# Step sizes and forget gates as fp32 products on four places of 32 columns, and the scan's heads later and further apart

## The reference, cut to what matters

```python
def mamba2_mixer(x, ln_g, in_w, conv_w, conv_b, dt_bias, a_log, d_skip, norm_g, out_w):
    zxbcdt = rms_norm(x, ln_g) @ in_w            # 1024 -> 5152 columns, the last 32 are dt
    z = zxbcdt[..., :D_INNER]
    xbc = zxbcdt[..., D_INNER:D_INNER + SSM_CONV_DIM]
    dt = zxbcdt[..., D_INNER + SSM_CONV_DIM:]
    xbc = jax.nn.silu(causal_dwconv(xbc, conv_w, conv_b))
    ...
    dt = jax.nn.softplus(dt + dt_bias)
    a = dt * (-jnp.exp(a_log))
    y = ssd_chunked(xs32 * dt[..., None], a, bm, cm)     # 32 heads in 4 groups, chunks of 128
    y = (y + xs32 * d_skip[:, None]).reshape(b, s, D_INNER) * jax.nn.silu(z)
    y = rms_norm(y, norm_g)                              # per group
    return y @ out_w

def fox_branch(q, k, v, f_logit, f_bias):
    log_f = jax.nn.log_sigmoid(f_logit + f_bias)         # 8 heads
    c = jnp.cumsum(log_f, axis=1)
    ...
        logits = q @ k * scale + c_q - c_k               # causal softmax, then @ v
```

## Time and profile before

| what | us |
|---|---|
| median of 3 timed runs (2403.49 to 2405.24) | 2404.54 |
| the profiled execution | 2402.46 |
| its span | 2400.7 |
| TensorE busy (99%) | 2376.7 |
| VectorE busy (58%) | 1403.3 |
| ScalarE busy (44%) | 1052.5 |
| GpSimd busy (15%) | 370.8 |

### The profile page before, as it was taken

How to read it: one execution, slowest core, us unless ns; L and a number is a source line. 1 busy time by engine, 2 the same in 40 slices (tenths; PEclk the granted TensorE clock), 3 DMA queues, 4 the chain that set the end, 5 groups by cost and what they waited for, 6 DMA issues and landing times.

```text
span 2400.7 us, 29668 instructions
## 1 busy us (share of the span) xinstructions
PE 2376.7 (99%) x11556; PEld 1930.8 (80%) x11556; DVE 1403.3 (58%) x2203; ACT 1052.5 (44%) x1803; POOL 370.8 (15%) x297
## 2 busy tenths in 40 slices
PE   8999999999999999999999999999999999999999
PEld 6777888888888877788888877787788877888887
DVE  6778776763665678766456557534555445443343
ACT  6654564442444677644234334324443334322223
POOL 0352252210111000121012100001211001110011
PEclk9999999999999999999999999999999999999999
DMA  4632223223223221232332332231243322223222
GB/s 164 110 92 79 81 74 101 88 86 109 96 82 127 72 71 54 75 102 94 98 102 87 99 131 72 78 102 61 68 132 128 114 97 88 88 95 99 105 78 90
DMA packets 74844, 226.19 MB, mean 94 GB/s; under 512 B 8144, under 2 KB 12368, under 8 KB 74576
## 3 DMA queue, kind: packets, MB, share of 16 engines
q1 hardware_dynamic: 70272, 215.90, 27.5%
q10 hardware_dynamic: 4432, 8.39, 2.0%
HBM read 215.87 MB, written 8.39 MB: 93 GB/s over the span
## 4 chain that ended last, share of the span: by engine, by line
PE 62%; DVE 1%; issue 0%; ACT 0%; POOLq 0%; POOL 0%; DVEq 0%
PE bank L1189 60%; PE bank L1193 1%; DVE t L2073 0%; ACT t L1595 0%; DVE t L2070 0%; DVE t L2081 0%; DVE t L2077 0%; ACT t L1598 0%; DVE t L2563 0%; POOLq L2862 0%; POOL t L2641 0%; DVEq L2862 0%; DVE t L2409 0%; DVE t L2078 0%; DVE t L2569 0%
## 5 line engine op out<-in xcount | busy, mean ns | idle before, releaser
L1189 PE MATMUL bank<-t 128*128 128x512 f32 (+4 forms) x11130 | 2352.3, 377 | 16.7 <-DVE t L2073 7.8
L1189 PEld LDWEIGHTS bank<-t 128*128 128x128 f32 (+2 forms) x11130 | 1888.0, 185 | 450.2 <-issue 80.0
L1595 ACT ACTIVATE t<-t 128x1024 fp32r<-128x1024 f32 (+6 forms) x634 | 539.3, 861 | 645.4 <-PE bank L1189 276.1
L2070 DVE TENSOR_TENSOR t<-t 128x1024 fp32r<-128x1024 f32 (+6 forms) x686 | 624.1, 920 | 260.6 <-ACT t L1595 254.5
L2641 POOL TENSOR_TENSOR t<-t 128x512 f32<-128x512 f32 (+4 forms) x217 | 329.0, 1523 | 1543.9 <-ACT t L1598 558.7
L1598 ACT ACTIVATE t<-t 128x512 f32<-128x512 f32 (+6 forms) x610 | 367.4, 616 | 450.3 <-DVE t L2070 301.2
L2070 DVE TENSOR_TENSOR t<-bank,t 128x512 f32<-128x512 f32 (+4 forms) x412 | 276.0, 674 | 451.9 <-PE bank L1189 441.5
L2073 DVE SCALAR_TENSOR_TENSOR t<-t 128x512 f32<-128x512 f32 (+4 forms) x493 | 364.0, 748 | 103.4 <-ACT t L1598 63.8
L1595 ACT ACTIVATE t<-bank 128x512 f32<-128x512 f32 (+4 forms) x151 | 72.2, 498 | 167.0 <-PE bank L1193 145.2
L2644 POOL TENSOR_SCALAR t<-t 128x128 f32<-128x128 f32 (+3 forms) x64 | 41.1, 649 | 476.8 <-ACT t L1595 246.1
L2073 DVE SCALAR_TENSOR_TENSOR t<-bank,t 128x512 f32<-128x512 f32 x56 | 38.5, 687 | 67.3 <-PE bank L1189 67.3
(11 more groups left out here) (30 smaller groups left out, 52.9 us busy)
## 6 DMA issues: line engine op xcount, KB each, us to landing
t<-in_w SPq DMA_DIRECT2D x304, 512.0 KB, 3.3
t<-in_w SPq DMA_DIRECT2D x48, 384.0 KB, 3.0
t<-in_w SPq DMA_DIRECT2D x56, 320.0 KB, 2.9
t<-in_w SPq DMA_DIRECT2D x28, 256.0 KB, 2.7
tab<-t ACTq DMA_DIRECT2D x1, 2560.0 KB
t<-in_x SPq DMA_DIRECT2D x8, 256.0 KB, 5.3
t<-tab SPq DMA_DIRECT2D x8, 256.0 KB, 3.9
spill<-t ACTq DMA_DIRECT2D x1, 2048.0 KB, 8.7
```

The lines of the kernel that those rows point to most:

```text
L1189: return eng.matmul(out, lhs, rhs, start=start, stop=stop, skip_group_check=loose)
L1595: return eng.activation(out, in_, ACT.Copy, scale=scale)
L2070: return eng.tensor_tensor(out, a, b, o)
```

## The change

The two narrow products get a form of their own, `thin`: one unit of 32 columns in one tick. Its weights are multiplied by the norm's gain in one VectorE step (in `cut`), without a split; the moving operand is the unsplit activation. The eight blocks go as plain fp32 products to four places of 32 columns, each place summing two blocks. The four partial sums lie on 128 partitions; VectorE scales them all, and the four transposes of `d1` and `f1` become products with four stacked identities in `l4`, which sum the places and turn the result at once. For the forget gates 32 columns are loaded and 8 used. `dt` moves from ahead of `in(0, 2)` to ahead of `in(0, 5)`, `fg` from the front of the mix stage to behind `sq 3`.

The first pair of group 0 may start 14 ticks after `stb` instead of 10, and pairs are 4 ticks apart instead of 3. Silu is whole on ScalarE for all `in` tiles of groups 0 to 2, 18 instead of 9; the table with Silu and Tanh is loaded at `in(2, 0)`, the one with Exp and Tanh at the first pair of groups 0 and 2.

```diff
@@ Plan
+    def thin(self, key, name, c0, src, nk, norm):
+
+        g = Group(key, False, src, 0, [], nk, 0, 32, S, norm=norm)
+        b = self.main_bank()
...
+        u = self.unit(name, 0, nk, c0, 32)
+        self.thin_units[u] = key[0]
+        g.units.append((u, 0, nk))
+        self.put(Piece(g, 0, 0, nk, True))
...
-                self.once("pair", (g, p), lambda g=g, p=p: self.past("stb", g, 10)
-                          and (p == 0 or self.past("pair", (g, p - 1), 3)),
+                self.once("pair", (g, p), lambda g=g, p=p: self.past("stb", g, 10 if g else 14)
+                          and (p == 0 or self.past("pair", (g, p - 1), 4)),
                           [(("s0", g, p), 0, 3), (("s1", g, p), 0, 3), (("bo", g, p), 3, 2), (("by", g, p), 5, 2)])
...
-                    self.feat(("dt",), "ssm_in", 5120, "n1", DC, ncol=32, norm="n1")
+                if g == 0 and i == 5:
+                    self.thin(("dt",), "ssm_in", 5120, "n1", DC, "n1")
...
-        self.feat(("fg",), "w_in", 3072, "nm", DC, ncol=8, norm="nm")
         feat(("sk",), 3080 + 512)
         feat(("sq", 0), ("swaq", 0))
         feat(("sv",), 3080 + 640)
         for i in range(1, 4):
             feat(("sq", i), ("swaq", i))
+        self.thin(("fg",), "w_in", 3072, "nm", DC, "nm")
@@ Kernel
     def silu_whole(self, key):
-        return key[:2] == ("in", 0) or key in (("in", 1, 0), ("in", 1, 1), ("in", 1, 2))
+        kind, g, i = key
+        return kind == "in" and g < 3
@@ tensor_program
+    def thin(p):
...
+        for first in range(0, g.nk, 4):
+            for q in range(4):
+                w.wait_ge(*K.ready(g.src, first + q))
+                t = mm(bank[32 * q:32 * q + 32, :], wg[:, first + q, :], buf.x[:, first + q, :], start=first == 0,
+                       stop=first + 4 == g.nk, loose=True)
...
             for j in range(NT):
-                t = turn(bank[:, 32 * j:32 * j + 32], buf.hd[0][0:32, j * P:j * P + P])
+                t = mm(bank[:, 32 * j:32 * j + 32], buf.hd[0][:, j * P:j * P + P], buf.l4[:, 32:64])
...
             for j in range(NT):
-                t = turn(bank[:, 8 * j:8 * j + 8], buf.ck[0][0:8, j * P:j * P + P])
+                t = mm(bank[:, 8 * j:8 * j + 8], buf.ck[0][:, j * P:j * P + P], buf.l4[:, 32:40])
@@ scalar_program
+            if i == 0 and g == 2:
+                load_set(SILU_AND_TANH)
...
-            if n == 0:
-                eng.add_instruction(mybir.InstLoadActFuncSet(name=eng.bass.get_next_instruction_name(), engine=eng.engine,
-                                                             act_func_set_id=EXP_AND_TANH))
+            if n in (0, 8):
+                load_set(EXP_AND_TANH)
@@ vector_program
-            tt(buf.hd[0][0:32, :], K.of(g.key)[0:32, :], buf.rsrow[0:32, :], MUL).then_inc(*leave(g.key))
+            tt(buf.hd[0][:, :], K.of(g.key)[:, :], buf.rsrow[:, :], MUL).then_inc(*leave(g.key))
...
+            eng.tensor_copy(buf.l4[r:r + 32, 32:64], buf.ident[r:r + 32, r:r + 32])
...
+        if u in plan.thin_units:
+            kind = plan.thin_units[u]
+            w.wait_ge(*sig.w[u % N_W].at(u // N_W + 1))
+            tt(K.thin_weights(kind), buf.raws[u % N_W][:, 0:n].rearrange("p (k n) -> p k n", k=DC),
+               pc("ssm_ln" if kind == "dt" else "mix", 0, DC).unsqueeze(2).to_broadcast([P, DC, 32]), MUL).then_inc(
+                *sig["cut"].up(u))
+            return
```

More of the change, by code:

```diff
@@ L30 @@
 N_MAIN = 3
-EXP_AND_TANH, LN_AND_EXP = 0, 6
+EXP_AND_TANH, LN_AND_EXP, SILU_AND_TANH = 0, 6, 18
 def t5_bucket(n):
@@ L282, in feat_steps @@
             self.unit_end[u] = ("bank", key) if first + k == nk else ("unit", u)
+        self.end[key] = self.T - 1
+        self.pending.append(g)
+    def thin(self, key, name, c0, src, nk, norm):
+        g = Group(key, False, src, 0, [], nk, 0, 32, S, norm=norm)
+        b = self.main_bank()
+        g.banks, self.main_last[b], self.bank[key] = [b], key, b
+        self.until(lambda: all(self.lo.get((src, i), 1 << 30) <= self.T for i in range(nk)), (key, src))
+        u = self.unit(name, 0, nk, c0, 32)
+        self.thin_units[u] = key[0]
+        g.units.append((u, 0, nk))
+        self.put(Piece(g, 0, 0, nk, True))
+        self.unit_end[u] = ("bank", key)
         self.end[key] = self.T - 1
@@ L805 @@
     "hi", "lo", "sq", "add_d", "add_p", "pow",
-    "pad", "tap0", "tap", "tanh", "silu", "silu_first", "dtx", "neg", "absn", "ealog", "expn", "ln1", "dt", "adt", "cs", "tail",
+    "pad", "tap0", "tap", "tanh", "silu", "silu_whole", "dtx", "neg", "absn", "ealog", "expn", "ln1", "dt", "adt", "cs", "tail",
     "ds", "csd", "csh", "xds", "stm", "sub", "edec", "gm", "yadd", "gate", "yn",
@@ L1079, in activated @@
     def activated(self, key):
-        return self.sig["silu_first" if self.silu_whole(key) else "silu"].at(*key)
+        return self.sig["silu_whole" if self.silu_whole(key) else "silu"].at(*key)
     def silu_whole(self, key):
-        return key[:2] == ("in", 0) or key in (("in", 1, 0), ("in", 1, 1), ("in", 1, 2))
+        kind, g, i = key
+        return kind == "in" and g < 3
     def u_before(self, key):
@@ L1133, in rms_row, with thin_weights @@
         return self.buf.rsrow
+    def thin_weights(self, kind):
+        t = self.buf.hd[1] if kind == "dt" else self.buf.ck[1]
+        return t[:, 0:DC * 32].rearrange("p (k n) -> p k n", k=DC)
     def hn_order(self):
@@ L1216, in features @@
                 t.then_inc(*sig["unit"].up(u))
+    def thin(p):
+        g = p.group
+        bank = take(g.key)
+        u = g.units[0][0]
+        w.wait_ge(*sig["cut"].at(u))
+        wg = K.thin_weights(g.key[0])
+        for first in range(0, g.nk, 4):
[3 more added lines that the diff above has]
+                       stop=first + 4 == g.nk, loose=True)
+        t.then_inc(*fill(g.key))
     def positions(p):
@@ L1581, in tensor_program @@
         if piece is not None:
-            if piece.group.tok:
+            if piece.group.units[0][0] in plan.thin_units:
+                thin(piece)
+            elif piece.group.tok:
                 positions(piece)
@@ L1705, in ssm @@
             w.wait_ge(*K.activated(old))
-            func(ACT.Tanh, buf.us[plan.u_n[key] % 3][:, 4:S + 4], buf.ZT[g % 2][:, i, :]).then_inc(*sig["tanh"].up(key))
+            z = buf.ZT[g % 2][:, i, :]
+            if K.silu_whole(key):
+                func(ACT.Silu, z, z, scale=2.0).then_inc(*sig["silu_whole"].up(*key))
+                continue
+            func(ACT.Tanh, buf.us[plan.u_n[key] % 3][:, 4:S + 4], z).then_inc(*sig["tanh"].up(key))
         for _ in at("once", T):
@@ L2048, in scalar_program @@
         for u in plan.split_at.get(T - 1, ()):
-            if 0 < u < len(plan.units):
+            if 0 < u < len(plan.units) and u not in plan.thin_units:
                 split(u)
@@ L2144, in evacuate @@
             w.wait_ge(*empty(("rb", "nm")))
-            tt(buf.ck[0][0:8, :], K.of(g.key)[0:8, :], buf.rsrow[0:8, :], MUL).then_inc(*leave(g.key))
+            tt(buf.ck[0][:, :], K.of(g.key)[:, :], buf.rsrow[:, :], MUL).then_inc(*leave(g.key))
         elif kind in ("sk", "sv"):
```

12 lines of the change are left out of this document (8 added, 4 removed).

## The result

The changed kernel takes 2432.66 us (median of 4 runs, 2432.53 to 2433.3) against 2404.01 us before (2403.37 to 2405.24, 4 runs): ratio 1.0119, 95% interval 1.0104 to 1.0134. It is 28.6 us slower; I had forecast 2404.8 with a range of 2393 to 2413. The profiled execution has a span of 2430.9 us, 30.2 more than before; its counterpart before was 2.1 us under the median of its timed runs.

The account below looks back on a forecast made before the run. TensorE's work plus its few standstills was taken as the bound. Terms -6.4 + 0.7 + 2.2 + 4.7 - 0.9 = +0.3 us on the median 2404.54 gave 2404.8 us, range 2393 to 2413.

Parts of the forecast that it names:

- Thin products: Step sizes and forget gates: four column places overlap fully, -3.2 us a site, -6.4 us in all.
- Nothing moves after the scan: Behind the scan: the last heads end earlier or within a tick of before, so no change there.
- The rest: GpSimd's wait in the scan goes, -0.9 us; after the scan, forget gates and extra copies at the start: 0.
- sign of being wrong: Whole kernel: new waits of TensorE outside 60 to 200 us, among others, would show the forecast wrong.
- The waits in front: First thin site, before tick 40: VectorE carries some 3 us more where TensorE waits 1.0 us; +0.7 us (0 to 1.5).
- The first pair: First heads of the scan: TensorE waits 6.4 us for ScalarE plus 2.5 of half clock, +2.2 us (0.4 to 4.7).
- Heads of group 1: Scan, group 1: table loads for silu make ScalarE's step longer than TensorE's; +4.7 us (-1.3 to 8).
- rival 3: Pairs (1,1) to (1,3): costlier table switches or late taps decide the scan; 2409 to 2417 us, chance 0.22.
- Group 2: Scan: four ticks between heads give GpSimd 1.4 us more a head and its wait goes, -0.9 us.
- The last head: End of the scan: the last heads end earlier or within a tick of before, with no cost.

Follow-up runs that it names:

- e4_phase: The changed kernel with one empty tick ahead of the first conv FFN: 2419.73 us.
- e7_thin_phase: e1_thin with one empty tick ahead of the first conv FFN: 2397.71 us.
- e1_thin: The changed kernel with the heads' ages and silu of before, so the thin products alone: 2407.11 us.
- e5_age14: The kernel before with only the first pair of group 0 at 14 ticks behind its states instead of 10: 2414.65 us.
- e11_no_silu: e4_phase with the silu of before, 15 table loads instead of 23: 2419.14 us.
- e14_all_banks: e4_phase with the planner told to keep the bank of bo one tick longer: 2412.66 us.
- e2_pairs: The kernel before with both ages of the changed one alone (first pair at 14 ticks, heads 4 apart): 2423.60 us.
- e10_best: e7_thin_phase with the first pair's table load one tick earlier and the weight split put behind its exponentials: 2394.94 us.
- e12_tabs_late: e5_age14 with the two table writes issued 28 and 12 ticks later: 2433.22 us, a single run.

## Why the prediction was wrong, point by point

**Thin products: right, mechanism and size.** I took 1.9 us a site for the products at four places and 1.0 for the identities. TensorE by form (shapes, count, busy us, mean ns), the answer to the earlier trace rows, gives 3.8 us for the thin products of both sites, and 1.0 for the identities of the step sizes:

```profile
L1211 PE MATMUL bank<-t 128*32 128x512 f32 x32 | 3.8, 598 | 0.0
...
L1211 PE MATMUL bank<-t 128*128 128x32 f32 x8 | 1.0, 265 | 0.0
```

That is 0.119 us for each instruction, 3.6 times as fast as one after another at the 0.43 that I had worked out for a single place. With the identities of the forget gates the work of both sites comes to -6.5 us (12.2 less, 5.7 more), against -6.4 in the sum. The 79% of full overlap that I had worked out from TensorE: Matmul & The Clock Gate of the Trainium skill, Part 3, gave 2.2 us a site; the trace has 1.9.

**"Nothing moves after the scan": wrong, and the largest step that failed.** It is the part of the prediction headed "The rest". I had taken three ticks earlier for everything as harmless and not asked what in the planner isn't free to move by three. The heads of the attention start on even ticks. The term that I left at nothing is 12.9 us by e4_phase and 9.4 by e7_thin_phase against e1_thin. The prediction's own sign of being wrong, new waits of TensorE outside 60 to 200 us, came up: the last head's at 366 us, and from 790 to 1010 us 10.5 us instead of 2.4.

**The waits in front:** +0.7 (0 to 1.5) was too small. I took the wait of 1.03 us at 69.18 for the one that would grow. It is gone in the changed kernel, and two others came: 0.56 us, and 2.71 us at 56.84, behind VectorE's evacuation of a tile. The clock fell behind the second, 1.7 us, for which I had no term: +3.7.

**The first pair: mechanism right, size right with some luck.** I forecast 5.9 to 8 us of waiting, taking 6.4, with the half clock 8.9, and for cause a split between Relus and exponentials that waits for a transfer. Measured are 7.12 and 2.6. Both ends of the wait came later than I had said: TensorE arrived at 103.1 instead of 99.5, ScalarE was at the table load at 102.09 instead of about 99, and the split waited until 108.73, where I had 103.8 to 106. That both moved by about as much, the 3.7 us lost in front among it, kept their difference; I hadn't foreseen it. And I compared with before as if that place had cost the same in any order. The single edit of the age costs 11.2 us when it stands alone (e5_age14).

**Heads of group 1: the sign right, one of two causes wrong, the size too small.** I put +4.7 on a ScalarE step of 9.4 to 10 us, lengthened by table loads. The place lost 8.8, and e11_no_silu, without the eight extra loads, loses as much there (6.9 of waits and 3.4 of clock from 180 to 230 us). ScalarE's steps were longer than I had taken: the Relus start at 175.49, 188.42 and 199.37, that is 12.9 and 10.9 us apart, with the waits for VectorE's taps among them. I had named these taps and given them no price; they stand ahead of the Relus without the loads too. A load does cost its 1.28 us and nothing behind it: the Relus start 0.01 us after the one at 102.09. So rival 3 was wrong in its first condition, the drain of 1380 ns that the Trainium skill (ScalarE: Activation LUTs, What ACT_TABLE_LOAD costs) gives for every switch; the trace doesn't agree with the page here. Its second condition, taps that come late, is what the traces show.

**Group 2: -0.9 was wrong.** Four ticks didn't free GpSimd; TensorE's waits for it there are 1.35 and 0.34, not gone.

**The last head, 366 us: missing.** It is the second step that failed, and it lies under the same sentence: "The last heads end earlier or within a tick of before". In ticks that is so, the last one starts at 182 in both kernels, but the features and VectorE's scaling of group 2 run three ticks ahead. The order rows showed `bo` of the first pair in the bank of its own `s0`, and I used that and didn't ask for the banks of the others. Ahead of the last head the shared bank and the scaling together cost 3.71 us and 2.9 of clock. e14_all_banks takes that away with one number.

**The range** had the two bounds of what I saw. It had none for what I had set to zero.

## What to carry to other kernels

When a change shortens a plan by some ticks, list what in the plan sits on a grid, in windows or in banks given out first-free, and compare each stage's distance to the features before and after; a stage that moved by another number of ticks than its neighbours isn't unchanged. An age or a distance in such a plan may look idle and yet keep an instruction ahead of a late transfer, or two results in two banks: read which queue and which bank its instructions get, and what they come to stand behind, before giving them more room. And an instruction that waits for a DMA costs what is queued behind it.

## What the runs showed of the hardware

- Four fp32 products of 32 columns side by side take 4 x 0.119 = 0.48 us at 512 columns. One alone is 0.43 us by the estimate from the earlier trace rows; no run has one alone.
- A table load of ScalarE takes 1.28 us, and the next instruction starts 0.01 to 0.02 us behind it.
- The clock fell to half after shorter waits than I had thought: after 2.40 us at 190.77 the stretch reads 0.66, in e2_pairs after 1.58 us at 226.79 it reads 0.74. It stayed at 1.00 in e10_best after 0.80, and before after 1.33.
- The length of the wait doesn't settle it. Behind 2.71 us at 56.84 two stretches of the changed kernel read 0.75 and 0.91; behind the same wait of 2.69 to 2.72 us in e1_thin, e7_thin_phase and e11_no_silu they read 1.00. Behind the 3.7 us of the last head, 365 to 375 us read 0.50 and 0.85 in the changed kernel and 0.66 and 1.00 in e11_no_silu. In the changed kernel the clock also fell with no wait ahead, 0.88 and 0.78 from 1460 to 1470 us. What decides is open.
- Table writes of 4 MB at the same time stretch the landing of 512 KB of weights from 3.3 to 15.4 us (50 to 105 us, e12_tabs_late and e5_age14).
